# A seventh weight slot, another order at the first norm, and half of four key units formed earlier

## The chip, the cores and the metric

The kernel runs on one core of a Trainium2 chip. The metric is the time of one execution on the device, in microseconds; lower is better. All data is float32. A weight piece is 128 partitions by 4096 elements, 2.1 MB, and 140 such pieces make up nearly all of the 304.6 MB that the program moves.

## The reference

Two layers over 256 tokens of width 1024, with a condition vector `c` that gives every sub-layer its shift, scale and gate. Layer 0 attends with forgetting gates (16 heads), layer 1 with differential attention (8 heads of twice 64), and each is followed by a mixture of 16 experts, of which every token uses 2. After each of the four sub-layers comes a norm.

```python
def modulate(x, shift, scale):
    return x * (1.0 + scale[:, None, :]) + shift[:, None, :]

def post_norm_residual(x, y, gate, g, b):
    return layer_norm(DEEPNORM_ALPHA * x + (1.0 + gate[:, None, :]) * y, g, b)
...
    for l in range(DEPTH):
        mod = ada_params(c, ada_w[l], ada_b[l])      # silu(c) @ w + b
        sh_a, sc_a, g_a, sh_f, sc_f, g_f = jnp.split(mod, 6, axis=-1)
        ...                                          # h = modulate(x, sh_a, sc_a); y = attention(h) @ w_o
        x = post_norm_residual(x, y, g_a, ln_attn_g[l], ln_attn_b[l])
        h = modulate(x, sh_f, sc_f)
        m = grouped_moe(h, router_w, router_b, moe_w_gate[l], moe_w_up[l], moe_w_down[l])
        x = post_norm_residual(x, m, g_f, ln_ffn_g[l], ln_ffn_b[l])
```

## The kernel before

**The weights.** All weights come through `ring`, six slots of one piece each. The list `pieces` sets one order for the whole program: four pieces of the first modulation (`N_ADA[0]`), two of keys (`N_K`), then values, queries and further modulation pieces (the groups `ada` 1 to 6, of which group 3 is the first one of `kv_ada_w`), two of the output product (`N_WO`), then 48 expert pieces (`N_MOE`), six for each of eight pairs of experts: gate, up, gate, up, down, down. Layer 1 repeats this. SyncE's block walks through this list (`load`, `expert_loads`); before each piece it waits on `used` of the slot, which TensorE or VectorE raises after the last reader of the piece that lay there. SyncE works strictly in this order, so a piece that waits for its slot holds up all that stand behind it. Two more slots (`spare` and `stream`, slots 6 and 7) serve while experts run: the buffer `spare` holds the norm's gain and bias rows (`lnw`) at other times, and `stream` holds the residual `xres` and the normed rows `h`. Hence the seventh expert piece waits on `x_ready` and the eighth on `res_mm`, which says that TensorE has read the residual.

**The first modulation.** `first_modulation` on TensorE takes the four pieces of `N_ADA[0]` one after the other: strip matmuls (L1465), a copy by ScalarE or VectorE, four column matmuls (L1470), then `idle_work` (L1453), matmuls whose result nobody reads. After two pieces half of the modulation's columns are known, and half of `hT` (the modulated input, feature by token) is formed by ScalarE and VectorE; after four the other half. Then `turned_units` (L1529) forms eight key units of eight matmuls each.

**A norm and what follows.** VectorE forms the normed rows of block 0 and of block 1 (128 tokens each) and raises `xn_r` twice for each. TensorE turns them (`turn_stream`, L1506), ScalarE and VectorE modulate the turned blocks (`turned`, four of eight features each), and TensorE forms the router's logits and the positions (`route`). GpSimd's `gained` (L595, L596) multiplies the rows by the gain and adds the bias; it raises `x_ready` once for each block. In `route`, TensorE adds the residual of block 1 (`residual(l, 1)`, L1694) ahead of the two small matmuls (L1683, L1684) from which VectorE counts where each expert's tokens begin. From there on come the gather (L1705), the residual of block 0 and the experts. The gain and bias rows of norm 0 are loaded by `norm_rows(0)` ahead of the output weights.

**The experts.** `experts` on TensorE takes the pairs in turn: gate and up of one expert (L1724, L1725), then of the other, and down (L1732, L1733). An expert with more than 64 tokens runs `overflow` (from L1746 on) for the rest, 32 at a time; ScalarE, VectorE and TensorE hand the data to each other there.

**The way into layer 1.** `turn_stream(1)` starts with five of eight parts of `mod_product(4)` (L1431), which needs all four pieces of modulation group 4, the last pieces before the keys of layer 1. `turn_mod(4, 0)` (L1480) then turns its row into columns, and the eight key units of layer 1 follow.

## Time and profile before

| | us |
|---|---|
| median of three runs | 898.19 (897.6 to 899.9) |
| the profiled execution | 900.95 |
| its span, first to last instruction | 899.3 |
| TensorE busy | 834.7 (93%) |
| VectorE busy | 376.0 (42%) |
| ScalarE, GpSimd busy | 127.1, 90.3 |
| data moved | 304.59 MB, 339 GB/s over the span |

The rows are those of the profiled execution. Its time is 1.7 us above its span, and 2.8 us above the median of the three runs. A busy TensorE is not one at its peak, since matmuls are pipelined. The profile cuts the span into 40 slices of 22.5 us; the row of GB/s gives what the transfers moved in each. An instruction's line number is that of the kernel before, and `PE` is TensorE, `DVE` VectorE, `ACT` ScalarE, `POOL` GpSimd, `SPq` SyncE's queue.

### The profile page before, as it was taken

Reading aid. Unit: us, or ns where it says so; the run is one execution under the profiler, and the core shown is the slowest. Engines: PE = TensorE matmul, PEld = TensorE weight load, DVE = VectorE, ACT = ScalarE, POOL = GpSimd, SP = SyncE. Lnnn points to the kernel's source line nnn. Section 1 sums busy time; section 2 is a strip of 40 time slices with the busy share of each in tenths; the row PEclk is TensorE's granted clock in tenths of the full one; section 3 lists DMA queues with packets and bytes.
Section 4 is the critical chain, followed back from the end, with each engine's and each line's share of the span. In section 5 each row is a group of like instructions: output and inputs, shape, how many; then the busy total and the mean of one; then the engine's idle time right before and its main releaser. Section 6 shows DMA issues by size and latency. Waiting matters only on the chain.

```text
span 899.3 us, 10792 instructions
## 1 busy us (share of the span) xinstructions
PE 834.7 (93%) x3730; PEld 393.0 (44%) x3730; DVE 376.0 (42%) x927; ACT 127.1 (14%) x341; POOL 90.3 (10%) x146
## 2 busy tenths in 40 slices
PE   6899999999998998899979999999999999889984
PEld 3584675435333333333328557654533333333331
DVE  2185867475211221222148688828521122212215
ACT  1001243011100000000010114611110000010010
POOL 1000000051110001011004000215111110000000
PEclk9999999999999999999999999999999999999998
DMA  8999982019999999999999799405499999999901
GB/s 352 431 421 426 399 329 95 1 59 431 426 428 426 425 427 426 427 426 426 425 384 419 299 426 425 175 0 213 163 406 424 428 424 427 426 427 426 392 12 47
DMA packets 23408, 304.59 MB, mean 339 GB/s; under 512 B 2720, under 2 KB 3232, under 8 KB 5280
## 3 DMA queue, kind: packets, MB, share of 16 engines
q1 hardware_dynamic: 22752, 303.14, 80.6%
q8 instruction: 47, 0.77, 0.3%
q10 hardware_dynamic: 576, 0.40, 0.1%
q14 instruction: 33, 0.27, 0.1%
HBM read 302.49 MB, written 1.05 MB: 338 GB/s over the span
## 4 chain that ended last, share of the span: by engine, by line
PE 68%; DMA 21%; DVE 8%; issue 2%; POOL 1%; ACT 1%; POOLq 0%; DVEq 0%; ACTq 0%
PE ps L1724 17%; DMA ring<-in_moe_w_up_dram 12%; PE ps L1732 7%; PE ps L1558 6%; PE ps L1529 6%; PE ps L1542 6%; PE ps L1642 5%; PE ps L1737 4%; DMA stream<-in_moe_w_up_dram 3%; DMA ring<-in_ada_w_dram 3%; DMA ring<-in_moe_w_down_dram 3%; PE ps L1453 1%; PE ps L1431 1%; PE ps L1705 1%; PE ps L1465 1%
## 5 line engine op out<-in xcount | busy, mean ns | idle before, releaser
L1724 PE MATMUL ps<-ring,hT 128*64 128x512 f32 x384 | 172.4, 599 | 11.8 <-DMA ring<-in_moe_w_up_dram 9.9
L1725 PE MATMUL ps<-ring,hT 128*64 128x512 f32 x384 | 172.7, 600 | 0.0
L1233 DVE TENSOR_TENSOR arena<-arena,ps 128x256 f32<-128x256 f32 x32 | 13.5, 421 | 233.8 <-ACT arena L802 126.8
L1724 PEld LDWEIGHTS ps<-ring,hT 128*64 128x64 f32 x384 | 51.1, 138 | 117.4 <-issue 117.4
L1732 PE MATMUL ps<-ring,arena 128*64 128x512 f32 x208 | 94.8, 599 | 0.0
L1733 PE MATMUL ps<-ring,arena 128*64 128x512 f32 x208 | 94.8, 598 | 0.0
L414 DVE SCALAR_TENSOR_TENSOR spare<-ring,csig,spare 128x512 f32<-128x512 f32 x112 | 86.1, 769 | 3.8
L1737 PE MATMUL ps<-arena 128*128 128x512 f32 x144 | 66.6, 605 | 3.2 <-DVE arena L1242 3.2
L1724 PE MATMUL ps<-spare,hT 128*64 128x512 f32 x128 | 58.9, 609 | 2.7 <-DMA stream<-in_moe_w_up_dram 2.5
L1725 PE MATMUL ps<-stream,hT 128*64 128x512 f32 x128 | 58.9, 610 | 0.0
L1529 PE MATMUL ps<-hT,ring 128*128 128x256 f32 x256 | 57.2, 386 | 1.5 <-ACT hT L680 1.5
L630 POOL COPY hT<-arena 128x512 f32 x32 | 19.7, 615 | 372.6 <-PE ps L1725 222.1
L1242 DVE TENSOR_TENSOR arena<-ps,gbc 64x512 f32<-64x512 f32 x64 | 43.9, 686 | 29.6 <-PE ps L1733 28.6
L1542 PE MATMUL ps<-ring,hT 128*128 128x512 f32 x128 | 55.9, 595 | 0.0
L1529 PEld LDWEIGHTS ps<-hT,ring 128*128 128x128 f32 x256 | 49.6, 194 | 8.5 <-ACT hT L680 1.6
L1725 PEld LDWEIGHTS ps<-ring,hT 128*64 128x64 f32 x384 | 51.2, 138 | 0.0
L1732 PEld LDWEIGHTS ps<-ring,arena 128*64 128x64 f32 x208 | 26.3, 136 | 48.9 <-issue 48.9
L1737 PEld LDWEIGHTS ps<-arena 128*128 128x128 f32 x144 | 25.9, 189 | 43.7 <-issue 43.7
L799 ACT ACTIVATE arena<-ps 128x512 f32<-128x512 f32 x16 | 9.6, 597 | 243.4 <-PE ps L1725 243.4
L1542 PEld LDWEIGHTS ps<-ring,hT 128*128 128x128 f32 x128 | 24.1, 190 | 30.8 <-issue 30.8
L1724 PEld LDWEIGHTS ps<-spare,hT 128*64 128x64 f32 x128 | 17.3, 140 | 38.7 <-issue 38.7
L587 POOL TENSOR_SCALAR st<-mv 128x1 f32<-128x1 f32 x8 | 1.8, 223 | 294.6 <-DVE mv L1064 294.6
(281 smaller groups left out, 1083.3 us busy)
## 6 DMA issues: line engine op xcount, KB each, us to landing
ring<-in_moe_w_down_dram SPq DMA_DIRECT2D x26, 2048.0 KB, 21.8
ring<-in_ada_w_dram SPq DMA_DIRECT2D x24, 2048.0 KB, 14.7
ring<-in_moe_w_gate_dram SPq DMA_DIRECT2D x24, 2048.0 KB, 18.4
ring<-in_moe_w_up_dram SPq DMA_DIRECT2D x24, 2048.0 KB, 21.3
spare<-in_moe_w_gate_dram SPq DMA_DIRECT2D x8, 2048.0 KB, 23.2
stream<-in_moe_w_up_dram SPq DMA_DIRECT2D x8, 2048.0 KB, 25.3
ring<-in_fox_w_in_dram SPq DMA_DIRECT2D x6, 2048.0 KB, 9.8
ring<-in_kv_ada_w_dram SPq DMA_DIRECT2D x4, 2048.0 KB, 13.8
```

Of the source, the lines that this page charges most:

```text
L414: ins = alu.scalar_tensor_tensor(out=dst, in0=w[:, k, :], scalar=csig[:, k:k + 1], in1=dst, op0=ALU.mult, op1=ALU.add)
L630: link(g.tensor_copy(xw[:, j, :, 0:CAP], xsT[:, :, bass.ds(first, CAP)]))
L1242: d.tensor_tensor(out[lo:lo + CAP, half], ps[part_, bank, :], gbc[part_, 1, half], ALU.mult).then_inc(done, 1)
L1529: mm = t.matmul(ps[:, u % 4, 0:S], wcols(piece)[:, k, cc * P:(cc + 1) * P], src[:, k, :], start=(k == 0), stop=(k == KC - 1))
L1542: mm = t.matmul(ps[:, u % 4, :], hT[:, k, b * P:(b + 1) * P], wcols(piece)[:, k, :], start=(k == 0), stop=(k == KC - 1))
L1558: mm = t.matmul(ps[:, 7, 0:S], wcols(n)[:, k, (c % 4) * P:(c % 4 + 1) * P], src[:, k, :], start=(k == 0), stop=(k == KC - 1))
L1642: mm = t.matmul(ps[:, 2 * b + s_, :], oT[l][:, k, b * P:(b + 1) * P], wcols(n)[:, k, :], start=(k == 0), stop=(k == KC - 1))
L1724: t.matmul(ps[0:CAP, bank, :], lhs(k), wcols(ng)[:, k, :], start=(k == 0), stop=(k == KC - 1))
L1725: mm = t.matmul(ps[CAP:P, bank, :], lhs(k), wcols(nu)[:, k, :], start=(k == 0), stop=(k == KC - 1))
L1732: t.matmul(ps[0:CAP, bank, :], lhs(f), wdown(n)[:, f, 0:512], start=(f == 0), stop=(f == 3))
L1733: mm = t.matmul(ps[CAP:P, bank, :], lhs(f), wdown(n)[:, f, 512:D], start=(f == 0), stop=(f == 3))
L1737: return t.matmul(ps[:, 2 * b + q, :], lhs[:, b * P:(b + 1) * P], yy[:, q * 512:q * 512 + 512], start=False, stop=True, skip_group_check=True)
```

## The change

- The second piece of layer 0's output weights, `N_WO[0][1]`, no longer goes to the ring. It is loaded in four quarters into buffers that are free then: the two norm rows `lnw`, `h` of block 1, and `fold`. All ring slots behind it shift by one: the first expert piece takes the slot of the last query piece.
- The gain and bias rows of norm 0 would lie in two of these quarters, so `norm_rows(0)` moves from ahead of the output weights to behind the third expert piece. It waits until the quarters have been read.
- `gained` takes block 0 first, and waits for that block's rows alone; `residual` waits for `x_ready` in that order, so that block 1's residual waits for both. `number_slots` moves behind `gained`.
- Half of the first key piece is loaded after the first two modulation pieces (`key_halves`), and `early_keys` forms the first four of eight steps of four key units between the pieces, in the place of `idle_work`. `turned_units` then starts these four at step 4.
- `turned`: ScalarE modulates all eight features of block 0 and four of block 1, VectorE the last four of block 1.
- In front of layer 1, `mod_product(4)` is split in other places, `idle_work` stands first, and `turn_mod(4, 0)` comes after the first key unit.
- In `overflow`, the two turning matmuls stand ahead of the fold, and one product with `gate_halves` (formed once for each layer) takes the place of two with `gbc`.

```diff
     SPARES = 2
+    HALVES = RING + SPARES
     SLOT, TURN = [], []
-    turns, free = [0] * (RING + SPARES), list(range(RING))
...
-        s = free.pop(0)
+        s = HALVES if n == N_WO[0][1] else free.pop(0)
         SLOT.append(s)
         TURN.append(turns[s])
         turns[s] += 1
-        free.append(s)
+        if s != HALVES:
+            free.append(s)
 
     COLS_C, COLS_ADA, COLS_LN, COLS_NORMG, COLS_BF = 0, KC, KC + 7 * 2 * KC, KC + 7 * 2 * KC + 8 * KC, KC + 7 * 2 * KC + 8 * KC + 1
...
+    HT_N = ((4, 4), (16, 8), (28, 12), (36, 20), (48, 24))
     ARENA = 9690
 
...
+            return [lnw[:, 0, :], lnw[:, 1, :], h[:, 1, :], fold[:, :, :].rearrange("p a n -> p (a n)")]
+
+        def out_rows(n, q):
+
+            if SLOT[n] == HALVES:
+                return [a_.rearrange("p (k n) -> p k n", k=2) for a_ in quarter_pieces()[2 * q:2 * q + 2]]
+            return [wcols(n)[:, k:k + 2, :] for k in (4 * q, 4 * q + 2)]
+
         def wdown(n):
             return room(n).rearrange("p (k n) -> p k n", k=4)
 
...
+            def load_quarters(n):
+
+                for s_ in range(2):
+                    sp.wait_ge(ht_ready[s_], HT_N[0][s_])
+                sp.wait_ge(f_steps, 1)
+                for q, part_ in enumerate(quarter_pieces()):
+                    sp.dma_start(part_, pieces[n][:, 1024 * q:1024 * q + 1024]).then_inc(full[HALVES], 16)
+
             def load(n):
...
                         w = (moe_w_gate, moe_w_up, moe_w_down)[j % 2 if j < 4 else 2]
+                        if l == 0 and 6 * i + j == 3:
+                            spent(sp, N_WO[0][1])
+                            norm_rows(0)
...
                         sp.dma_start(room(n), w[l, e]).then_inc(full[SLOT[n]], 16)
+
+            def key_halves(q):
+
+                return room(N_K[0][0])[:, 2048 * q:2048 * q + 2048]
...
                     gate_bias(1)
-                if n == N_WO[0][0]:
-                    norm_rows(0)
                 if 2 <= n < RING:
                     landed(sp, n - 2)
-                load(n)
+                if n == 2:
+                    sp.dma_start(key_halves(0), pieces[N_K[0][0]][:, 0:2048]).then_inc(k_half, 16)
+                if n == N_K[0][0]:
+                    sp.dma_start(key_halves(1), pieces[n][:, 2048:4096]).then_inc(full[slot(n)], 16)
+                else:
+                    load(n)
             expert_loads(0)
             sp.wait_ge(xn_r, 4)
             gate_bias(2)
...
                 pool.wait_ge(lw_in, 32 * (norm + 1))
-                pool.wait_ge(xn_r, 4 * (norm + 1))
-                for b in (1, 0):
+                for b in range(NB):
+                    pool.wait_ge(xn_r, 4 * norm + 2 * b + 2)
                     link(g.tensor_tensor(xres[:, b, :], h[:, b, :], lnw[:, 0, :], ALU.mult))
                     g.tensor_tensor(xres[:, b, :], xres[:, b, :], lnw[:, 1, :], ALU.add).then_inc(x_ready, 1)
 
...
             inv_std(0)
+            gained(0)
             number_slots(0)
-            gained(0)
             windows(0)
...
                 spent(act, N_ADA[0][2 * half])
-                a.activation(parts[:, 2 * half, :], ps[:, 2 * half, :], ACT.Copy).then_inc(part_ev[0], 1)
+                a.activation(parts[:, 2 * half, :], ps[:, 6, :], ACT.Copy).then_inc(part_ev[0], 1)
                 first_turned(half)
 
...
                 act.wait_ge(cols_r, m + 2)
                 for b in range(NB):
-                    if m == 2 and b:
-                        mod_row_out(4)
-                    act.wait_ge(ht_mm, 4 * norm + 2 * b + 1)
-                    for k in range(4):
+                    for k in range(KC if b == 0 else 4):
+                        if k % 4 == 0:
+                            act.wait_ge(ht_mm, 4 * norm + 2 * b + k // 4 + 1)
                         modulated(hT[:, k, b * P:(b + 1) * P], turned_bank(b, k), m, k).then_inc(ht_ready[0], 1)
...
 
-                norm = M_NORM[m]
-                for b in range(NB):
-                    dve.wait_ge(ht_mm, 4 * norm + 2 * b + 2)
-                    for k in range(4, KC):
-                        modulated(hT[:, k, b * P:(b + 1) * P], turned_bank(b, k), m, k).then_inc(ht_ready[1], 1)
+                dve.wait_ge(ht_mm, 4 * M_NORM[m] + 4)
+                for k in range(4, KC):
+                    modulated(hT[:, k, P:2 * P], turned_bank(1, k), m, k).then_inc(ht_ready[1], 1)
 
...
                 landed(dve, n)
-                w = wcols(n)[:, 4 * q:4 * q + 4, :]
-                d.tensor_tensor(w, w, gbc[:, 0, 512 * s_:512 * s_ + 512].unsqueeze(1).broadcast_to([P, 4, 512]),
-                                ALU.mult).then_inc(wo_r, 1)
+                g_ = gbc[:, 0, 512 * s_:512 * s_ + 512].unsqueeze(1)
+                if SLOT[n] != HALVES:
+                    w = wcols(n)[:, 4 * q:4 * q + 4, :]
+                    d.tensor_tensor(w, w, g_.broadcast_to([P, 4, 512]), ALU.mult).then_inc(wo_r, 1)
+                    return
+                for at, w in enumerate(out_rows(n, q)):
+                    ins = d.tensor_tensor(w, w, g_.broadcast_to([P, 2, 512]), ALU.mult)
+                    if at:
+                        ins.then_inc(wo_r, 1)
+                    else:
+                        link(ins)
 
             def diff_norm(hd):
...
                     dve.wait_ge(ga_mm, KC * l + k + 1)
                     modulated(xsT[:, k, 0:NSLOT], ps[:, gather_bank(k), :], (1, 4)[l], k).then_inc(xs_ev[1], 1)
                 overflow_tables(l)
+                for q, rows in enumerate((slice(0, 64), slice(64, P))):
+                    link(d.tensor_copy(gate_halves[rows, :], gbc[rows, 1, 512 * q:512 * q + 512]))
                 for i in range(PAIRS):
                     n0 = N_MOE[l] + 6 * i
                     q = i + 8 * l
...
                         for strip in range(4):
-                            mm = t.matmul(ps[32 * strip:32 * strip + 32, at, :], crep[:, 2 * strip + k, :],
+                            mm = t.matmul(ps[32 * strip:32 * strip + 32, 6 + at % 2, :], crep[:, 2 * strip + k, :],
                                           wcols(n)[:, 2 * strip + k, :], start=(k == 0), stop=(k == 1))
                     mm.then_inc(used[slot(n)], 1)
                     pe.wait_ge(part_ev[at % 2], at // 2 + 1)
                     for kk in range(4):
-                        mm = t.matmul(ps[:, 4 + at, kk:kk + 1], parts[:, at, kk * P:(kk + 1) * P],
+                        one = 4 * (at // 2) + kk
+                        mm = t.matmul(ps[:, 4 + at % 2, one:one + 1], parts[:, at, kk * P:(kk + 1) * P],
                                       strips[:, 0:1], start=True, stop=True)
                     mm.then_inc(col_mm, 1)
-                    if at < 3:
-                        idle_work((4, 6, 3)[at], at + 1)
+                    if at == 0:
+                        idle_work(4, 7)
+                    if at == 1:
+                        idle_work(1, 3)
+                        for s_ in range(2):
+                            pe.wait_ge(ht_ready[s_], HT_N[0][s_] // 2)
+                        pe.wait_ge(k_half, 16)
+                        early_keys(range(3))
+                    if at == 2:
+                        early_keys(range(3, 4))
+
+            def early_keys(us):
+
+                for u in us:
+                    for k in range(KC // 2):
+                        t.matmul(ps[:, u, 0:S], wcols(N_K[0][0])[:, k, u * P:(u + 1) * P], hT[:, k, :],
+                                 start=(k == 0), stop=False)
 
             def turn_mod(gi, bank):
 
...
                 if norm == 1:
-                    mod_product(4, range(0, 5))
+                    idle_work(3, 7)
                 for b in range(NB):
                     if b and norm == 0:
                         mod_product(3, range(0, 2))
                     if b and norm == 1:
-                        mod_product(4, range(5, KC))
+                        mod_product(4, range(0, 3))
                     if b and norm == 2:
                         zeroed((0, 1, 0))
                     for s_ in range(2):
                         pe.wait_ge(xn_r, 4 * norm + 2 * b + s_ + 1)
-                        if norm == 1 and b and s_:
-                            pe.wait_ge(mod_row, 4)
                         for k in range(4 * s_, 4 * s_ + 4):
                             mm = t.transpose(turned_bank(b, k), h[:, b, k * P:(k + 1) * P], ident[:, :])
                         mm.then_inc(ht_mm, 1)
+                if norm == 1:
+                    mod_product(4, range(3, KC))
 
             def stream_turned(m):
...
                     for cc in range(4):
+                        if u == UNITS0 + 1:
+                            turn_mod(4, 0)
                         unit_free(u)
-                        for k in range(KC):
+                        for k in range(KC // 2 if u < 4 else 0, KC):
                             mm = t.matmul(ps[:, u % 4, 0:S], wcols(piece)[:, k, cc * P:(cc + 1) * P], src[:, k, :],
                                           start=(k == 0), stop=(k == KC - 1))
...
 
-                pe.wait_ge(x_ready, 2 * NB * l + 2 - b)
+                pe.wait_ge(x_ready, 2 * NB * l + b + 1)
...
                         with pe.Fori(b, b + n) as g:
-                            k = g * 8
+                            k = g * 7
                             pe.wait_ge(o_win, g + 1)
                             landed(pe, N_MOE[l] + 6 * i + 2 * j)
                             landed(pe, N_MOE[l] + 6 * i + 2 * j + 1)
                             gate_up_strips(i, j).then_inc(o_pe, 1)
+                            pe.wait_ge(o_dve, k + 3)
+                            for bb in range(NB):
+                                mm = t.transpose(ps[:, 7, bb * P:(bb + 1) * P], oput[:, bb, :], ident[:, :])
+                            mm.then_inc(o_pe, 1)
                             pe.wait_ge(o_act, g * 2 + 1)
-                            pe.wait_ge(o_dve, k + 3)
                             for q in range(4):
                                 mm = t.matmul(ps[:, 6, q * 2 * OCAP:(q + 1) * 2 * OCAP], ogu[:, q * P:(q + 1) * P],
                                               fold_strips[:, :], start=True, stop=True)
                             mm.then_inc(o_pe, 1)
...
             turn_stream(1)
             stream_turned(2)
-            turn_mod(4, 0)
```

In SyncE's queue, the pieces around the first experts stood so before (`kv_ada_w` is modulation group 3, `usedN` is the wait for slot N):

```order
L484 DMA ring<-in_kv_ada_w_dram 128x4096 [waits used3]
L511 DMA spare<-in_ln_attn_g_dram 128x1024
L511 DMA spare<-in_ln_attn_b_dram 128x1024
L484 DMA ring<-in_fox_w_o_dram 128x4096 [waits used4]
L484 DMA ring<-in_fox_w_o_dram 128x4096 [waits used5]
L498 DMA ring<-in_moe_w_gate_dram 128x4096 [waits used0]
L498 DMA ring<-in_moe_w_up_dram 128x4096 [waits used1]
L498 DMA ring<-in_moe_w_gate_dram 128x4096 [waits used2]
```

And now, in the same place:

```order
L508 DMA ring<-in_kv_ada_w_dram 128x4096 [waits used3]
L508 DMA ring<-in_fox_w_o_dram 128x4096 [waits used4]
L501 DMA spare<-in_fox_w_o_dram 128x1024 [waits f_steps,ht_ready_dve,ht_ready_act]
L501 DMA spare<-in_fox_w_o_dram 128x1024
L501 DMA stream<-in_fox_w_o_dram 128x1024
L501 DMA fold<-in_fox_w_o_dram 128x1024
L525 DMA ring<-in_moe_w_gate_dram 128x4096 [waits used5]
L525 DMA ring<-in_moe_w_up_dram 128x4096 [waits used0]
L525 DMA ring<-in_moe_w_gate_dram 128x4096 [waits used1]
L542 DMA spare<-in_ln_attn_g_dram 128x1024 [waits used8]
L542 DMA spare<-in_ln_attn_b_dram 128x1024
L525 DMA ring<-in_moe_w_up_dram 128x4096 [waits used2]
```

The norm rows have moved past both output pieces and three expert pieces, two of which wait for slots 0 and 1, where modulation group 3 lies.

On TensorE, between the second and the fourth piece of the first modulation, stood before:

```order
L1470 MATMUL ps<-strips,arena 128x1 x3
L1453 MATMUL ps<-maskf,ones 128x384 x6
L1465 MATMUL ps<-ring,crep 32x512 [waits full2]
L1465 MATMUL ps<-ring,crep 32x512 x7
L1470 MATMUL ps<-strips,arena 128x1 [waits part_ev_act]
L1470 MATMUL ps<-strips,arena 128x1 x3
L1453 MATMUL ps<-maskf,ones 128x384 x3
L1465 MATMUL ps<-ring,crep 32x512 [waits full3]
```

And now:

```order
L1512 MATMUL ps<-strips,arena 128x1 x3
L1494 MATMUL ps<-maskf,ones 128x384
L1530 MATMUL ps<-hT,ring 128x256 [waits k_half,ht_ready_dve,ht_ready_act]
L1530 MATMUL ps<-hT,ring 128x256 x11
L1506 MATMUL ps<-ring,crep 32x512 [waits full2]
L1506 MATMUL ps<-ring,crep 32x512 x7
L1512 MATMUL ps<-strips,arena 128x1 [waits part_ev_act]
L1512 MATMUL ps<-strips,arena 128x1 x3
L1530 MATMUL ps<-hT,ring 128x256 x4
L1506 MATMUL ps<-ring,crep 32x512 [waits full3]
```

Sixteen key matmuls (`hT,ring`) stand where eight of nine idle ones stood. In the trace each of these instructions has two records.

## Rows read from the trace of the kernel before

**Rows 1.** The page's row of data moved, one number for each of 40 slices.
```profile
GB/s 352 431 421 426 399 329 95 1 59 431 426 428 426 425 427 426 427 426 426 425 384 419 299 426 425 175 0 213 163 406 424 428 424 427 426 427 426 392 12 47
```

**Rows 2.** Stretches, window: length, busy us of PE, PEld, DVE, ACT, POOL, clock, DMA share, GB/s.
```profile
216.80:460.40 243.60, 224.70 (x986) 80.59 (x986) 55.99 (x136) 17.84 (x35) 20.00 (x35) 0.99 1.01 426
460.40:641.10 180.70, 174.10 (x759) 109.03 (x760) 125.48 (x301) 46.42 (x152) 30.56 (x39) 0.99 0.67 274
784.40:899.30 114.90, 96.29 (x450) 33.69 (x450) 31.22 (x66) 7.63 (x16) 7.31 (x14) 0.94 0.63 265
34.80:38.20 3.40, 3.02 (x7) 2.48 (x8) 0.78 (x4) 0.33 (x1) 0.00 (x0) 0.50 1.04 443
461.50:464.80 3.30, 3.30 (x23) 1.01 (x16) 1.32 (x2) 0.00 (x0) 0.00 (x0) 0.50 1.00 423
```

**Rows 3.** Timeline of SyncE's queue: start us, us, queue, line, transfer.
```profile
117.00 25.01 SPq L484 DMA_DIRECT2D ring<-in_fox_w_o_dram  x2
...
197.49 0.33 SPq L498 DMA_DIRECT2D ring<-in_moe_w_gate_dram  x1
...
215.91 0.33 SPq L498 DMA_DIRECT2D stream<-in_moe_w_up_dram  x1
224.82 0.33 SPq L498 DMA_DIRECT2D ring<-in_moe_w_gate_dram  x1
```

**Rows 4.** Line 498's transfer issued at 197.49 us.
```profile
DMA to landing us min/median/max: 7.4/7.4/7.4
```

**Rows 5.** Line 498's transfer issued at 224.82 us.
```profile
DMA to landing us min/median/max: 20.8/20.8/20.8
```

**Rows 6.** Timeline, GpSimd, 189 to 199 us: first and last of four gain products.
```profile
189.13 2.38 POOL L595 TENSOR_TENSOR stream<-stream,spare 128x1024 f32<-128x1024 f32 x1 [0.88 <-DVE stream L1072]
...
196.36 2.42 POOL L596 TENSOR_TENSOR stream<-stream,spare 128x1024 f32<-128x1024 f32 x1
```

**Rows 7.** Timeline, TensorE, 200 to 217 us.
```profile
200.95 1.88 PE L1694 MATMUL ps<-stream,identa 128*128 128x512 f32 x4
...
216.84 0.61 PE L1724 MATMUL ps<-ring,hT 128*64 128x512 f32 x1 [0.96 <-POOL hT L631]
```

**Rows 8.** The chain of waits, 9 to 40 us: start us, us, engine, line.
```profile
16.59 1.90 PE ps L1465 x16
...
20.31 3.98 PE ps L1453 x12
24.29 1.90 PE ps L1465 x16
...
27.91 2.04 PE ps L1453 x6
29.96 1.90 PE ps L1465 x16
```

**Rows 9.** Timeline, TensorE: the eight key units of layer 0.
```profile
35.18 29.37 PE L1529 MATMUL ps<-hT,ring 128*128 128x256 f32 x128 [1.51 <-ACT hT L680]
```

**Rows 10.** The chain of waits, 434 to 480 us.
```profile
433.99 26.35 DMA ring<-in_ada_w_dram
...
460.48 6.20 PE ps L1431 x40
466.67 1.02 PE ps L1506 x8
467.69 2.83 PE ps L1431 x24
...
473.52 0.63 PE ps L1480 x4
```

**Rows 11.** Timeline, VectorE: the last share of modulation group 5.
```profile
503.33 5.48 DVE L414 SCALAR_TENSOR_TENSOR spare<-ring,csig,spare 128x512 f32<-128x512 f32 x7
```

**Rows 12.** The chain of waits, 515 us: the sum over those shares.
```profile
515.52 1.00 PE ps L1446 x8
```

**Rows 13.** Waits of TensorE, 643 to 899 us: in total, times, longest.
```profile
PE ps L1724 <- DMA ring<-in_moe_w_up_dram: 3.0, 1, 3.0
```

**Rows 14.** The chain of waits, 844 to 875 us: the second of two gate products.
```profile
861.88 0.71 DVE arena L1271
```

**Rows 15.** Timeline, VectorE: the modulation products after norm 2.
```profile
616.67 2.63 DVE L898 TENSOR_SCALAR hT<-ps,modc 128x128 f32<-128x128 f32 x8
```

More of the change, by code:

```diff
@@ L105, in build @@
     SPARES = 2
+    HALVES = RING + SPARES
     SLOT, TURN = [], []
-    turns, free = [0] * (RING + SPARES), list(range(RING))
+    turns, free = [0] * (RING + SPARES + 1), list(range(RING))
     for n in range(len(pieces)):
@@ L251, in build @@
         ogu = mrow[:, 1, :]
-        full = [sem(f"full{i}") for i in range(RING + SPARES)]
-        used = [sem(f"used{i}") for i in range(RING + SPARES)]
+        full = [sem(f"full{i}") for i in range(RING + SPARES + 1)]
+        used = [sem(f"used{i}") for i in range(RING + SPARES + 1)]
         res_mm = sem("res_mm")
@@ L830, in _ @@
             turned(2)
+            mod_row_out(4)
             us = proj_units(1)
@@ L1269, in overflow @@
                             dve.wait_ge(o_pe, g * 5 + 4)
-                            for q, rows in enumerate((slice(0, 64), slice(64, P))):
-                                d.tensor_tensor(oy[rows, :], ps[rows, 7, :], gbc[rows, 1, 512 * q:512 * q + 512],
-                                                ALU.mult).then_inc(o_dve, 1)
+                            d.tensor_tensor(oy, ps[:, 7, :], gate_halves, ALU.mult).then_inc(o_dve, 1)
                             dve.wait_ge(o_pe, g * 5 + 5)
```

39 lines of the change are left out of this document (21 added, 18 removed).

## The prediction

> **What bounds the kernel now.** I read the data moved by slice first, then the stretches, then SyncE's queue, and only then the chain of waits. The row of GB/s [rows 1] shows three kinds of time: transfers at about 426 GB/s, a gap in the slices from 135 to 202 us (95, 1 and 59), and another in layer 1. From 216.8 to 460.4 us the 16 DMA engines are busy for the whole stretch (share 1.01, 426 GB/s) while TensorE leaves 19 of 243.6 us free [rows 2]: layer 0's experts are bound by transfers, and one piece takes 2.1 MB / 426 GB/s = 4.9 us. Layer 1's attention (460.4 to 641.1 us) moves only 274 GB/s and keeps TensorE busy: that stretch, like layer 0's attention, belongs to TensorE. In layer 1's experts TensorE waits only once for weights, 3.0 us [rows 13].
>
> So a change counts here if it lets the transfers of layer 0's experts start earlier or run without a hole, or if it shortens TensorE's chain elsewhere. SyncE's queue shows why they start late: between the output weights (117.00 and about 25 us later) and the first expert piece (197.49) no transfer is issued, since all six slots are taken until TensorE has finished modulation group 3 [rows 3].
>
> **The first modulation.** Before, the strips of its second to fourth piece start at 16.59, 24.29 and 29.96 us, and the first key unit at 35.18 [rows 8, 9]. From the last strips to that unit is 5.2 us; the same way for the first half puts the first four features of `hT` at 16.59 + 5.2 = 21.8 us. The eight units are 64 matmuls, 128 records in 29.37 us, so 0.46 us for a matmul. Twelve early ones run from 21.8 to 27.3, so the third piece's strips start at 27.3 in place of 24.29. The key half ahead of it costs the piece 1.05 MB / 426 GB/s = 2.5 us; it was there by 24.29, so now by 26.8, which is hidden. To the fourth piece it was 5.67 us, of which 2.04 idle matmuls; with four key matmuls (1.8) in their place its strips start at 27.3 + 5.5 = 32.8. It was there by 29.96 and so now by 32.5. The first unit starts at 38.0, and 48 matmuls are left, 22.0 us: 60.0 in place of 64.55. That is 4.5 us. I take 4.0, as the transfers behind are no earlier than before and run at their limit up to about 110 us [rows 1]. Bounds: 0, if the added waits eat it, and 6.0, if TensorE isn't at the lower clock here, which it was from 34.8 to 38.2 us (0.50, so 1.2 GHz) [rows 2].
>
> The quartered output piece makes four products of two; a product over 128x512 takes 0.71 us [rows 14], and the elements are as many as before, so it costs between 0 and 0.7 us, and I take 0.2. TensorE's release of modulation group 3, and with it the first issues of expert weights, comes at 197.49 - 4.0 + 0.2 = 193.7 us.
>
> **The seventh slot and the norm rows.** The first expert piece now lands in the gap, which is worth 4.9 us. But the gain and bias rows stand behind two pieces that wait for slots 0 and 1, so they too are issued after 193.7. A piece issued into an empty queue lands 7.4 us later [rows 4]: pieces two and three at 201.1 and 206.0, the rows (1.05 MB, 2.5 us) at 208.5. GpSimd's four products took from 189.13 to 196.36 + 2.42, 9.65 us [rows 6], and end at 218.2. `residual(0, 1)` now waits for both blocks, and it stands on TensorE ahead of the counting matmuls. It ran at 200.95 [rows 7] and will run at 218.2: 17.2 us later. Behind it are queued the counts, the gather, the second residual and all experts; nothing of the router's chain on VectorE can pass. The first expert matmul moves from 216.84 [rows 7] to 234.1.
>
> TensorE stands still for some 20 us there. After the one long wait in front of layer 1 it ran at 0.50, 1.2 GHz, in 461.5 to 464.8 us [rows 2]. From the old residual to the first expert lie 15.9 us of which about two thirds are matmuls; running all of these at half speed would add up to 10 us, none 0. I take 2.5, nearest to a spell like the 3.3 us of that row with some work behind it, and get 236.6. The Trainium skill ("TensorE: Matmul & The Clock Gate", section "What's actually happening") has it that the throttled clock is the default and sustained activity releases it. By that rule the restart is slow, as in the row at 461.5; without it the sum below would come to -1.0 in place of +1.5.
>
> The eight slots hold pieces one to eight; the ninth needs the first one's slot. TensorE gave that back 224.82 - 216.84 = 7.98 us after the first expert matmul [rows 3, 7], so now at 244.6. By then the queue has run dry (eight pieces' work ended long before; the eighth waits for `res_mm`, 215.91 [rows 3], now 235.7, and lands at 243.1). The ninth lands at 244.6 + 7.4 = 252.0. Before, it landed 20.8 us after 224.82, at 245.6 [rows 3, 5]. From there on both versions are bound by transfers of the same number: TensorE needs about 26 us for six pieces and the transfers 29.4, and it has caught up before the end. So layer 0's weights end 6.4 us later, although 4.0 + 4.9 us were put in ahead. Of the 19 us that TensorE had free, most are used up.
>
> **In front of layer 1.** The last piece of modulation group 4 landed at 433.99 + 26.35 = 460.34, and the first key unit started at 473.52 + 0.63 = 474.15, 13.8 us later [rows 10]. Now only the 64 instructions of the modulation (6.20 + 2.83) and one block's turns (1.02) stand in between, 10.05 us: 3.8 us less, with `turn_mod`'s 0.63 paid after the first unit: -3.2. The new `idle_work` lies in the wait. The cover: VectorE's shares of group 5 stay tied to their transfers, and the last ends at 508.8, against 515.52 where TensorE reads them [rows 11, 12]; 6.7 - 3.2 = 3.5 us of slack are left. If that is gone, up to 3.2 us come back.
>
> **The small ones.** `overflow` loses one 0.71 us product on the way of TensorE [rows 14]. Two such runs of layer 1 lie behind the last wait for weights, so -1.4, and the moved turns another -0.1. The one in layer 0 isn't at the bound. Four of the eight VectorE products of 2.63 us after a norm [rows 15] move to ScalarE, 1.3 us at most; TensorE fills most of that time with other matmuls, so I take 0.2 for norm 2. Norm 2's gain products start earlier, but TensorE has eight idle matmuls (`zeroed`) ahead of that residual: 0.
>
> **The sum** against the profiled execution (900.95 us, span 899.3): +6.4 - 3.2 - 1.5 - 0.2 = +1.5 us. On the median of the three runs, 898.19, that is 899.7.
>
> **The rivals.** (1) The seventh slot pays. If the norm rows landed soon after their issue, not behind two pieces, `x_ready` would come at about 210 and the ninth piece at 243; if nothing waited at all, at 239. The totals are then -7.5 and -11.5 us, 890.7 and 886.7. For it: the rows are small. Against it: a transfer into a filled queue landed after 20.8 us, one into an empty queue after 7.4 [rows 4, 5], so they take turns, and the program's order puts the rows behind slots 0 and 1 whatever the queue does. (2) Slower, by the restart. Every microsecond that TensorE's way from the residual to the first returned slot loses is a microsecond of the whole, since the transfers then wait for it. It decides from 1.2 us above my 2.5; at the lower clock for half of that way it costs 5.5, so 902.7, and for all of it 10, so 907. For it: 20 us of standing still, followed by short matmuls with waits between them. Against it: in the two rows at 0.50 one short spell was all. (3) Somewhat faster: no slow spell at the restart and none in the key units, -2.5 - 2.0 on my sum, 895.2.
>
> **How the numbers follow.** This kernel's measurement can tell about 0.3%, 2.7 us. My forecast with its neighbourhood, 896 to 902, has a chance of 0.52; the slower restart beyond that 0.30; rival (3) 0.10; rival (1) 0.08. Within the first case some weight is past +2.7 (above 900.9), so: faster 0.14, within 0.3% 0.48, slower 0.38. The likeliest case's own range is 896 to 903. The range for 8 in 10 reaches to rival (3) and to the half of the slow restart: 893.5 to 905.
>
> **What would show it.** In the changed profile: no matmul to speak of on TensorE from about 197 to 218 us, its residual waiting for GpSimd, and GpSimd waiting for the norm rows' transfer until about 208; a first expert piece landed by 150; the first expert matmul near 236; a hole in the transfers at about 230 to 245; the first key unit at 38, the units' end at 60; 10 us from the last piece of group 4 to layer 1's first key unit. I am wrong if that residual doesn't wait, if TensorE can't catch up with the transfers before 460 us, or if the shares of group 5 become a wait.

## The result, and the profile after

The changed kernel takes 907.49 us (median of 11 runs, 903.96 to 912.62) against 899.6 of the kernel before in the same comparison (11 runs, 895.35 to 904.95): ratio 1.0091, 95% interval 1.0065 to 1.0117. It is slower, and outside my range of 893.5 to 905. The profiled execution took 911.69 us (span 910.0; before 900.95 and 899.3), so 10.7 us are to be found.

The page's rows of clock, DMA share and data moved, in 40 slices:

```profile
PEclk9899999995999999989999999999999999999988
DMA  9999992039499999999998899505289999999901
GB/s 353 403 421 429 400 369 94 1 125 421 175 431 425 427 425 426 427 421 427 423 426 366 356 427 414 210 1 217 104 351 427 425 428 425 426 426 428 422 39 47
```

The slice at about 228 to 250 us, 426 before [rows 1], moves 175: a hole that was not there. SyncE's queue (columns as in [rows 3]) shows how it comes about:

```profile
140.88 0.33 SPq L525 DMA_DIRECT2D ring<-in_moe_w_gate_dram  x1
196.59 0.33 SPq L525 DMA_DIRECT2D ring<-in_moe_w_up_dram  x1
196.96 0.43 SPq L525 DMA_DIRECT2D ring<-in_moe_w_gate_dram  x1
197.44 0.43 SPq L542 DMA_DIRECT2D spare<-in_ln_attn_g_dram  x1
...
221.22 0.33 SPq L525 DMA_DIRECT2D spare<-in_moe_w_gate_dram  x1
238.26 0.33 SPq L525 DMA_DIRECT2D stream<-in_moe_w_up_dram  x1
247.16 0.33 SPq L525 DMA_DIRECT2D ring<-in_moe_w_gate_dram  x1
```

One expert piece is issued in the gap. The other two wait for their slots until 196.59, and only then come the norm rows. The ninth piece goes out at 247.16, before at 224.82. GpSimd and TensorE's waits from 200 to 475 us:

```profile
211.72 2.34 POOL L629 TENSOR_TENSOR stream<-stream,spare 128x1024 f32<-128x1024 f32 x1 [24.42 <-DMA spare<-in_ln_attn_b_dram]
...
218.86 2.34 POOL L630 TENSOR_TENSOR stream<-stream,spare 128x1024 f32<-128x1024 f32 x1
```

```profile
PE ps L1754 <- POOL stream L630: 21.0, 1, 21.0
PE ps L1816 <- DMA ring<-in_moe_w_down_dram: 2.3, 1, 2.3
```

GpSimd waits for the bias row's transfer, and TensorE's residual waits 21.0 us for GpSimd. This wait is called the hold from here on. The stretches (columns as in [rows 2]) show the same hole, and the lower clock beside it:

```profile
198.00:221.00 23.00, 2.21 (x6) 0.66 (x4) 1.17 (x8) 0.00 (x0) 9.12 (x4) 0.60 0.99 412
221.00:240.00 19.00, 17.09 (x56) 10.89 (x58) 11.62 (x40) 4.39 (x5) 2.85 (x5) 0.85 0.55 222
203.00:226.60 23.60, 5.35 (x13) 3.29 (x14) 0.67 (x4) 0.00 (x0) 9.84 (x5) 0.50 1.01 423
```

Followed along the program, the changed kernel is later than before by: -0.9 us at SyncE's first issue behind modulation group 3; +20.3 at `residual(0, 1)` (221.25); +22.3 at the first expert matmul (239.19); +9.4 at the landing of modulation group 4's last piece (469.70), as the transfers' free time in layer 0 is used up; +8.3 at the end of layer 1's key units (510.06); +13.1 at layer 1's second residual (654.08); +10.7 at the end.

The rise from 8.3 to 13.1 is at norm 2. Here VectorE's normed rows and GpSimd's gain products, first of the kernel before, then of the changed one:

```profile
615.60 1.15 DVE L1072 TENSOR_SCALAR stream<-stream,mv,st 128x512 f32<-128x512 f32 x2 [1.08 <-POOL st L588]
```

```profile
616.89 2.36 POOL L595 TENSOR_TENSOR stream<-stream,spare 128x1024 f32<-128x1024 f32 x1 [0.88 <-DVE stream L1072]
```

```profile
623.88 4.98 DVE L1112 TENSOR_SCALAR stream<-stream,mv,st 128x512 f32<-128x512 f32 x2 [1.08 <-POOL st L622]
```

```profile
623.75 2.34 POOL L629 TENSOR_TENSOR stream<-stream,spare 128x1024 f32<-128x1024 f32 x1
626.16 2.41 POOL L630 TENSOR_TENSOR stream<-stream,spare 128x1024 f32<-128x1024 f32 x1
628.94 2.35 POOL L629 TENSOR_TENSOR stream<-stream,spare 128x1024 f32<-128x1024 f32 x1 [0.36 <-DVE stream L1112]
```

Before, GpSimd starts once VectorE has finished. Now it starts 0.13 us ahead of it, and the same two VectorE instructions take 4.98 us, not 1.15. Each lasts until a GpSimd product has ended (626.09, 628.58) and 0.3 us more. No row calls this a wait: it is hidden in the duration. TensorE's turns hang on it. They wait 1.90 and 1.84 us for these rows, and a stretch at 0.50 follows (629.45 to 632.87 us), in which four idle matmuls take 3.57 us, where four take 1.88 us in the kernel before:

```profile
626.42 0.66 PE L1561 MATMUL ps<-ident,stream 128*128 128x128 f32 x4 [1.90 <-DVE stream L1112]
628.92 0.66 PE L1561 MATMUL ps<-ident,stream 128*128 128x128 f32 x4 [1.84 <-DVE stream L1112]
629.41 3.57 PE L1760 MATMUL ps<-arena,ones 128*128 128x512 f32 x4
```

So the loss at norm 2 has two parts: the rows, 3.8 us longer, and the lower clock behind them, 1.4 us between the rows' end and the router's first matmul (4.05 us, before 2.70), for which the idle matmuls have to end. The steps behind that are 0.3 us shorter than before.

### The profile page after: what moved, and what is told of

It reads as the page before. It is cut to its first block, busy times and chain, and to the rows that moved or that the text cites. A ratio compares the mean times of both kernels' runs of the same rounds, so it can differ in the third digit from the quotient of the medians.

```text
span 910.0 us, 10780 instructions
## 1 busy us (share of the span) xinstructions
PE 838.6 (92%) x3720; PEld 393.6 (43%) x3720; DVE 370.3 (41%) x918; ACT 131.5 (14%) x353; POOL 90.9 (10%) x146
## 3 DMA queue, kind: packets, MB, share of 16 engines
HBM read 302.49 MB, written 1.05 MB: 334 GB/s over the span
## 4 chain that ended last, share of the span: by engine, by line
PE 82%; DMA 7%; DVE 6%; POOL 2%; issue 1%; ACT 1%; SPq 0%; POOLq 0%; DVEq 0%; ACTq 0%
PE ps L1784 22%; PE ps L1792 11%; PE ps L1617 6%; PE ps L1797 6%; PE ps L1601 6%; PE ps L1588 6%; PE ps L1701 5%; DMA ring<-in_moe_w_up_dram 3%; DMA ring<-in_moe_w_down_dram 3%; DMA spare<-in_ln_attn_b_dram 2%; PE ps L1472 1%; PE ps L1760 1%; PE ps L1765 1%; PE ps L1845 1%; PE ps L1871 1%
## 5 line engine op out<-in xcount | busy, mean ns | idle before, releaser
L428 DVE SCALAR_TENSOR_TENSOR spare<-ring,csig,spare 128x512 f32<-128x512 f32 x112 | 84.2, 752 | 3.8
L1588 PE MATMUL ps<-hT,ring 128*128 128x256 f32 x224 | 52.0, 395 | 1.5 <-ACT hT L714 1.5
L1588 PEld LDWEIGHTS ps<-hT,ring 128*128 128x128 f32 x224 | 44.3, 199 | 8.9 <-ACT hT L714 1.6
```

The lines of the kernel that those rows point to most:

```text
L428: ins = alu.scalar_tensor_tensor(out=dst, in0=w[:, k, :], scalar=csig[:, k:k + 1], in1=dst, op0=ALU.mult, op1=ALU.add)
L1588: mm = t.matmul(ps[:, u % 4, 0:S], wcols(piece)[:, k, cc * P:(cc + 1) * P], src[:, k, :], start=(k == 0), stop=(k == KC - 1))
```

## The experiments

All ratios are to the kernel before, in runs on the same chip, with 95% intervals.

**Norm rows first.** In `expert_loads(0)`:

```
-                        if l == 0 and 6 * i + j == 3:
+                        if l == 0 and 6 * i + j == 1:
                             spent(sp, N_WO[0][1])
                             norm_rows(0)
```

> The changed kernel, with the two norm rows issued as soon as the output piece in the seventh slot is spent (about 185 us), ahead of expert pieces two and three in SyncE's program, not behind them. Theory (the hold in front of the experts): the rows land near 193, GpSimd's four products end near 202, residual(0, 1) runs at 201 to 203 instead of 221.3, the first expert matmul at 217 to 219 instead of 239.2, the last piece of modulation group 4 lands at 454 to 457 instead of 469.7; total 892 to 896, so 12 to 15 us below the changed kernel and a few us below the kernel before. Rival 1 (the loss is TensorE's lower clock, whatever the rows do): the residual moves but the total stays within 4 us of 907. Rival 2 (layer 0's experts are now TensorE's own bound): the weights' end moves by less than 5 us, total 901 or more.

Measured: 893.74 us, ratio 0.9933 (0.9905 to 0.9962); faster than both kernels. SyncE's queue:

```profile
184.48 0.33 SPq L542 DMA_DIRECT2D spare<-in_ln_attn_g_dram  x1
...
196.40 0.33 SPq L525 DMA_DIRECT2D ring<-in_moe_w_up_dram  x1
...
224.81 0.33 SPq L525 DMA_DIRECT2D ring<-in_moe_w_gate_dram  x1
```

The residual runs at 199.86, the first expert at 216.83, group 4 ends at 454.11, 15.6 us earlier. Both rivals fall. The seventh slot gives its piece's time once nothing holds: 454.11 against 460.34 before is 6.2 us, of which 1.1 are the earlier first issue (196.40, before 197.49) and 5.1 the piece. This is read from the traces; no run has the seventh slot as its only change.

**The norm order undone.** GpSimd's blocks in the order (1, 0) after all four halves, `number_slots` ahead of `gained`, `residual` waiting on `2 * NB * l + 2 - b`.

> The changed kernel with the norm order undone: GpSimd numbers the slots first and takes block 1 before block 0 after all four normed quarters are there, and residual(l, 1) waits for one block alone. Theory: at norm 0 residual(0, 1) needs two products less, 4.7 us, so 216.5 in place of 221.3 and layer 0's end 4 to 5 us earlier; at norm 2 VectorE's two normed rows of block 1 take 1.1 us again, not 5.0, and the router starts 4 to 5 us earlier; together 8 to 10 us, total 897.5 to 900. Rival 1 (only the hold behind pieces two and three counts, norm 2's long rows are made up for later): 4 to 5 us, 903. Rival 2 (clock): within 2 us of 907.5.

Measured: 899.46, ratio 0.9993 (0.9974 to 1.0012). The residual runs at 215.27, group 4 ends at 463.70 (469.70), and norm 2's rows take 1.15 us again. Both parts count. Of the 6.0 us at the residual 4.5 belong to the order: the first issue behind modulation group 3 was itself 1.5 us earlier in this trace (195.08).

**One line of it.**

```
-                for b in range(NB):
-                    pool.wait_ge(xn_r, 4 * norm + 2 * b + 2)
+                pool.wait_ge(xn_r, 4 * (norm + 1))
+                for b in range(NB):
```

> The changed kernel with one line altered: GpSimd's gain products wait for all four normed quarters, and so don't start beside VectorE's normed rows of block 1; the blocks' order and its place ahead of the slot numbers stay. Theory (GpSimd's products and VectorE's normed rows hold each other up at norm 2): the rows take 1.1 us in place of 5.0, the router of layer 1 starts 4 to 5 us earlier against the end of the attention, nothing changes at norm 0 where the rows' transfer is last; total 902.5 to 904. Rival (the long rows come from something else, or the gain is eaten by the later products, which residual(1, 1) now waits for): total within 1.5 us of 907.5.

Measured: 904.4, ratio 1.0046 (1.0025 to 1.0067), 4 us less than the changed kernel's ratio gives. Layer 0 is unaltered (group 4 ends at 469.73), and VectorE's two rows are short:

```profile
623.50 1.00 DVE L1112 TENSOR_SCALAR stream<-stream,mv,st 128x512 f32<-128x512 f32 x2 [1.08 <-POOL st L622]
```

**Both** (called the mixture below): norm rows first, norm order undone.

> Both: the norm rows issued ahead of pieces two and three, and the norm order undone. Theory, by the sum of the two: residual(0, 1) near 200, as in the kernel before, the first expert near 216, the last piece of modulation group 4 at 454 to 456, norm 2 without the stretch: 888 to 891, so 9 to 11 us below the kernel before (ratio 0.988 to 0.990). Rival (the two gains are not additive, since TensorE becomes the bound of layer 0's experts once the hold is gone): 893 to 896.

Measured: 888.56, ratio 0.9880 (0.9850 to 0.9910). The gains of the rows' place (0.0158 of the ratio) and of norm 2 (0.0045, from the run with one line altered) add up: 0.9888 is their sum. The part of the norm order that lay in the hold goes with the hold.

**Late rows in the kernel before.** No seventh slot; `norm_rows(0)` is taken from ahead of the output weights and put behind the third expert piece.

> The kernel before, with one thing of the change and no seventh slot: its two norm rows are issued behind the first three expert pieces, not ahead of the output weights. Theory (the hold alone makes the loss in layer 0): the rows land near 215, GpSimd's first two products end near 219.5, residual(0, 1) runs there in place of 200.95, TensorE runs at the lower clock around it, the ninth piece is issued at 243 to 246 in place of 224.8 and group 4's last piece lands at 466 to 470 in place of 460.3; total 6 to 10 us above the kernel before, 906 to 910. Rival (the loss came from the quartered piece in the seventh slot or from the new pieces' order): the hold is caught up by the experts' end, total within 2 us of 900.

Measured: 909.26, ratio 1.0090 (1.0063 to 1.0117): this one move makes a loss as large as the whole change.

```profile
195.84 0.33 SPq L500 DMA_DIRECT2D ring<-in_moe_w_gate_dram  x1
...
197.16 0.51 SPq L513 DMA_DIRECT2D spare<-in_ln_attn_g_dram  x1
...
246.51 0.33 SPq L500 DMA_DIRECT2D ring<-in_moe_w_gate_dram  x1
```

The residual runs at 220.78 and group 4 ends at 469.10. The early expert piece of the changed kernel is worth nothing while the hold is there.

**The new norm order alone, in the kernel before.**

> The kernel before with the norm order of the change alone: GpSimd takes block 0 as soon as its two halves are normed, ahead of the slot numbers, and residual(l, 1) waits for both blocks. The norm rows are there early, so here the products can meet VectorE's normed rows of block 1 at both norms. Theory (they hold each other up wherever they meet): the two rows take 4 to 5 us in place of 1.1 at norm 0 (near 187 us) and at norm 2 (near 616 us); TensorE's last product of modulation group 3, and with it the first issue of expert weights, comes 3 to 5 us later than 197.5, and the total rises by 7 to 10 us, to 907 to 910. Rival 1 (only norm 2 has it): 4 to 5 us, 904 to 905. Rival 2 (the long rows of the changed kernel came from the other edits): within 1.5 us of 900.

Measured: 909.5, ratio 1.0115 (1.0084 to 1.0145). With the rows there early, the two engines meet at norm 0 as well; VectorE's and GpSimd's rows there:

```profile
188.99 4.97 DVE L1072 TENSOR_SCALAR stream<-stream,mv,st 128x512 f32<-128x512 f32 x2 [1.07 <-POOL st L588]
```

```profile
188.85 2.34 POOL L595 TENSOR_TENSOR stream<-stream,spare 128x1024 f32<-128x1024 f32 x1
191.27 2.41 POOL L596 TENSOR_TENSOR stream<-stream,spare 128x1024 f32<-128x1024 f32 x1
```

The first expert weights go out at 203.96, 6.5 us later than before; I had expected 3 to 5. Of the 6.5 us 1.2 were there before the norm (188.99 against 187.83, first column of these rows; the key units of layer 0 had ended 1.2 us later, at 65.72), and 3.8 are the rows. A stretch at 0.50 (191.0 to 197.8 us) that begins in the middle of this may be the last 1.5; I didn't test that. At norm 2 the same rows are as long and no stretch at 0.50 follows; from their start to the second residual it takes 3.5 us more than before, not 4.9.

**The lower clock around the hold.** Two runs. In the first I meant to fill the hold with matmuls on zeros, and put them in a wrong place:

```
                 pe.wait_ge(tot_r, l + 1)
                 zeroed((1, 1))
+                if l == 0:
+                    zeroed((1,) * 11)
```

> The changed kernel with eleven more matmuls on zeros (1.86 us each, 20.4 us) on TensorE ahead of residual(0, 1), so that it is busy through the hold; the hold itself stays. Theory (the restart's lower clock is a small part of the loss): no stretch at 0.50 from 202 to 226 us, residual(0, 1) still at 221.3, the first expert matmul 1.5 to 2.5 us earlier than 239.2, and layer 0's end as much: total 905 to 906. Rival (the lower clock is most of the loss): 6 us or more, total 901.5 or less.

Measured: 916.97, ratio 1.0186 (1.0160 to 1.0212). They stood behind the residual, not ahead of it as the expectation says, so this run tells nothing of the clock. But it is a dose of the other step: TensorE's way from the residual to the first returned slot is made longer. First expert +6.8 us against the changed kernel (246.04), ninth issue +6.8 (254.01), group 4's end +6.8 (476.54). In each of the six kernels with the hold that end comes 222.5 to 222.8 us after the ninth issue; in the kernel before, whose queue was full, 235.5.

In the second they are in the hold:

```
                 if l == 0:
                     mod_product(3, range(4, KC))
-                    zeroed((6, 7, 6, 7))
+                    zeroed((6, 7) * 13)
```

> The changed kernel with 22 more matmuls on zeros directly ahead of residual(0, 1), 0.93 us each by the row of the four that stand there (3.70 us), so 20.5 us: TensorE is busy through the hold, and the hold itself stays. (In hold_busy eleven of them stood behind that residual, 10 us of work on the way to the first expert.) Theory (the restart's lower clock is a small part of the loss): residual(0, 1) stays at 219 to 221.5, no stretch at 0.50 around it, the first expert matmul 17 to 18 us behind it rather than 17.9 plus, so 1.5 to 3 us earlier than in the changed kernel against its residual (239.19 - 221.25 = 17.9, before 15.9), and layer 0's end as much: total 904 to 906. Rival (the lower clock is most of the loss): 901.5 or less.

Measured: 906.08, ratio 1.0073 (1.0049 to 1.0096). The stretch is at full clock, and the residual still waits:

```profile
198.00:220.00 22.00, 19.75 (x47) 8.51 (x46) 0.00 (x0) 0.00 (x0) 9.53 (x5) 1.00 1.02 425
```

```profile
195.02 22.58 PE L1760 MATMUL ps<-arena,ones 128*128 128x512 f32 x52
219.86 1.98 PE L1754 MATMUL ps<-stream,identa 128*128 128x512 f32 x4 [2.25 <-POOL stream L630]
```

From residual to first expert it is 15.8 us, as before the change (15.9), not 17.9. So, in the traces, the lower clock costs 2.1 of the 22.3 us, and the wait itself the rest. In time the run is not told apart from the changed kernel (1.0073 and 1.0091, the intervals overlap), but it is far from the 901.5 us or less that the rival asked for.

**Parts of the mixture undone.** Early key units: the key piece comes whole, the idle matmuls are back, all eight units run behind the modulation. The line that forms them:

```
-                        for k in range(KC // 2 if u < 4 else 0, KC):
+                        for k in range(KC):
```

> The faster mixture (norm rows first, old norm order) without the early key units: the first key piece comes whole, TensorE's idle matmuls are as in the kernel before, and all eight units run behind the first modulation. Theory (the transfers behind the key units take up their gain): the units end 1 to 6 us later than the mixture's 63.3 or at the same time, but TensorE's last matmul of modulation group 3 comes only 0.5 to 1.5 us later, and so does the end: 889 to 890.5 against 888.6. Rival (my forecast's term, 4 us of units are 4 us of the whole): 892 to 893.

Measured: 889.87, ratio 0.9871 (0.9848 to 0.9893), the same as the mixture's 0.9880. The units end at 64.4 (63.3), the first issue is at 197.38 (196.34): what little the early units gain in the mixture's trace, 1.1 us, arrives in full, and the run doesn't test what becomes of a larger gain. The other traces do. Up to 1.7 us ahead of the kernel before the first issue follows the units' end (the units 1.2 us ahead and the issue 1.3 in the run with one line altered, both 1.7 with the late rows). With the units 4.1 to 6.4 us ahead (the two runs for the hold, and the norm order undone), the first issue was only 2.2 to 2.4 us ahead.

The work in front of layer 1 in its old order (the first lines of the edit):

```
                 if norm == 1:
-                    idle_work(3, 7)
+                    mod_product(4, range(0, 5))
...
```

> The faster mixture with the work in front of layer 1 in its old order: modulation group 4's products in bank 7 around the first block's turns, ScalarE's row before the second block, VectorE's fold of group 3 and turn_mod before the first key unit. Theory: the mixture starts its first key unit 10.3 us after group 4's last piece has landed, the kernel before 13.8; undone it is 13 to 14 again, less 0.6 for turn_mod, so the total rises by 2.5 to 4 us, to 891 to 892.5. Rival (VectorE's shares of group 5 hang on their transfers and take it back): 888 to 889.5.

Measured: 892.0, ratio 0.9912 (0.9890 to 0.9933). The intervals overlap; the trace has the key units' end 39.7 us after group 4's last piece, in the mixture 38.6, where it is 36.6 when TensorE arrives early enough (norm rows first). So the trace shows 1.1 us of the 2.5 to 4 that I expected, and the time can't settle it.

The overflow's steps as before:

> The faster mixture with the overflow's steps as before: two down products of 64 rows, and the turned places behind the folded strips. Theory: 0.7 us a round for the second product and up to 0.5 for the order; two rounds of layer 1 stand at TensorE's bound and layer 0's ones partly, so 1.4 to 3 us in all, 890 to 891.5. Rival (other matmuls cover it): within 0.7 us of 888.6.

Measured: 890.65, ratio 0.9892 (0.9863 to 0.9920): not told from the mixture by time. In the traces the first round of layer 1, with no lower clock in it, takes 12.24 us undone and 11.19 with the change, so 1.05 us a round.

**The mixture with its first gaps filled:** `idle_work(2, 3)` ahead of the early key units, and after the fourth piece `idle_work(2, 6)`.

> The faster mixture with three idle matmuls more in the first modulation: one ahead of the early key units and two ahead of the others, in TensorE's gaps of 0.8 and 1.5 us. Theory: what is gained there lies in front of transfers that run back to back, so at most 1.3 us reach the first issue of expert weights even if the two stretches at 0.50 (21.4 and 38.5 us) go: 887 to 889, same as the mixture's 888.6 within its spread. Rival (the gaps bring the lower clock, and it costs the whole 5 us): 884 to 885.

Measured: 887.29, ratio 0.9850 (0.9823 to 0.9877), the lowest, though its interval overlaps the mixture's. No stretch at 0.50 is left before 84 us, and the key units end at 58.1, where I had forecast 60.0. TensorE's and VectorE's rows:

```profile
20.94 5.45 PE L1532 MATMUL ps<-hT,ring 128*128 128x256 f32 x24
...
37.13 20.99 PE L1590 MATMUL ps<-hT,ring 128*128 128x256 f32 x96
...
74.82 7.13 PE L1603 MATMUL ps<-ring,hT 128*128 128x512 f32 x16 [0.35 <-DMA ring<-in_fox_w_in_dram]
85.02 10.05 PE L1603 MATMUL ps<-ring,hT 128*128 128x512 f32 x16 [3.06 <-DVE arena L1016]
```

```profile
79.78 0.49 DVE L426 TENSOR_SCALAR spare<-ring,csig 128x512 f32<-128x512 f32 x1 [4.54 <-DMA ring<-in_ada_w_dram]
80.30 2.33 DVE L428 SCALAR_TENSOR_TENSOR spare<-ring,csig,spare 128x512 f32<-128x512 f32 x3
...
84.74 0.22 DVE L1016 COPY arena<-arena 72x128 f32<-72x128 f32 x1
```

The units end at 58.1, 6.4 us ahead of the kernel before. But VectorE waits 4.54 us for a modulation piece, forms half of its share, and only then the forget gate (L1016), for which TensorE waits 3.06 us. The first issue comes at 197.76, no earlier than before (in this run a stretch at 0.50 from 84.1 us stretches the next units from 7.13 to 10.05). In the run with the norm order undone, which had no lower clock there either, the units also ended at 58.2 and the first issue came at 195.08: of 6.4 us, 2.4 were left. That these waits for the transfers are what takes the rest is read from the rows; no run removes them.

## Why the prediction was wrong

**The hold was right in kind and nearly in size.** Residual behind the slots' release: +24.5 us forecast (218.2 - 193.7), 24.7 measured. From there to the first expert 18.4 against 17.9, clock 2.5 against 2.1, to the ninth issue 8.0 against 8.0. That the transfers never catch up from there was right too (group 4 ends 214.8 us after the ninth's landing before, 215.2 now). I had taken that end at +6.4; it came at +9.4, because all of it counts from the first issue.

**The first step that failed: "That is 4.5 us. I take 4.0, as the transfers behind are no earlier than before".** The sentence names the reason and then discounts it by 0.5. Measured: -0.9. The two parts of the error: in the changed kernel's trace the key units ran partly at 0.50 (38.9 to 45.8 us; their 96 records took 23.90 us, not 20.99), and so did the early ones (21.9 to 25.3 us; 24 records in 6.96 us, not 5.43), so they ended only 0.8 us earlier; and where they ran at full clock, 4.0 of 6.4 us were lost behind them, where the transfers had no free time [rows 1]. By the run without these stretches the first issue would have been 2.4 us earlier at full clock, and not 3.8: 1.4 us of the error are the way behind the units, 1.5 the clock. I asked whether the key pieces were there in time, but not what VectorE does with the pieces behind them. The sum's error from this is +3.0.

**The second: "Norm 2's gain products start earlier ... : 0".** It cost 4.9 us in the trace, a stretch at the lower clock included; in time, altering that one line gives back 0.45% or 4 us. I looked at who waits for the products (nobody, behind `zeroed`), not at what they run beside. The trace of before shows the effect. Its chain of waits has

```profile
196.59 2.35 DVE rc L1118
```

beside GpSimd's product of 196.36 [rows 6], and in the changed kernel, where GpSimd is idle at that time, the same step (L1158, 194.63 us) takes 0.29. The Trainium skill states the rule ("SBUF — State Buffer", section "SBUF: two separate sides"): VectorE, in its two-port modes or with two inputs from SBUF, and GpSimd lock a shared pair of ports for a whole instruction; whichever starts first has it, and the other one blocks. By that rule each of the two rows ends one short step behind one of GpSimd's products; the trace agrees (0.28 us behind 626.09 and behind 628.58), though no row names the mode of these rows. With the 4.9 us in the sum the forecast would have been 904.6.

**Third, in front of layer 1: "-3.2".** Measured: -1.1. The 10.05 us were counted from the last piece's landing, as if TensorE were ready then, which it was before. After the hold TensorE itself is late. Its waits for weights in layer 0 are down to one of 2.3 us (at 384.7), and group 4's last piece (469.70) finds it at the experts' end:

```profile
466.58 3.67 PE L1797 MATMUL ps<-arena 128*128 128x512 f32 x8 [1.61 <-DVE arena L1282]
470.08 2.10 PE L1494 MATMUL ps<-maskf,ones 128*128 128x384 f32 x6
...
477.29 4.50 PE L1472 MATMUL ps<-ring,crep 128*32 128x512 f32 x40
481.72 3.72 PE L1588 MATMUL ps<-hT,ring 128*128 128x256 f32 x16
```

The idle matmuls (L1494), meant for the wait, run behind it, and the first key unit starts 12.0 us after the landing. Where it is early, the edit gives more than I took: first key unit 8.3 us after the landing with the norm rows first, 13.8 before. The shares of group 5, the cover that I had named, did not become a wait: VectorE had them at 518.7, and TensorE read them at 523.7.

**The overflow, "-1.5":** 1.05 us a round in the trace for a round at full clock, two rounds in layer 1. Their sum can't be read from the changed kernel, whose last round met a stretch at 0.50 (868.4 to 875.2) and took 14.08 us, before 13.83. All behind norm 2 gave -2.4, of which some 1.6 are such a stretch of the kernel before (785.7 us) that isn't there now. Such stretches come and go between the traces, so I call that part luck.

The four differences, +3.0, +2.1, +5.1 and -0.9, make up the 9.2 us between the forecast sum of +1.5 and the +10.7 measured, but for rounding.

**The rivals.** Rival (2), slower, had the right sign, 902.7 to 907, for the wrong reason: it put the price on the clock after the hold, and 2.1 us of clock is all there was behind it. Rival (1), the seventh slot pays, did not come about in this kernel: the rows, issued at 197.44 and 197.91, landed at 210.1 and 211.7, as the main case had it. What it said would follow if nothing waited can be compared with the experiments: the ninth piece at 239 and -11.5 us. With the norm rows first it landed at 239.4, and the time by the ratio was -6.0 us with norm 2's loss in it; with the norm order undone as well it landed at 239.3, and the time was -10.8.

## What to carry to other kernels

When a load moves behind others in a queue, its place costs what those others wait for, not their bytes: here two small rows behind two waiting pieces cost all that the slot gained and more, and moving them up two places turned a loss of 0.9% into a gain of 0.7%. Before an instruction of GpSimd is moved earlier, look at what VectorE runs at that time; a block shows as long durations, not as waits. A gain on TensorE in front of transfers that run back to back may be worth only its first part: here 1.7 us passed whole, and of 6.4 us 2.4 were left.

## What the hardware showed beside this

The lower clock came and went between executions of the same code: the two early stretches at 0.50 (about 21.5 to 25 and 38.5 to 45.5 us) were there in six of the nine profiled kernels whose first modulation is the changed kernel's; two had only one, at 37.5 and 37.8 us for 3.4 us, and one had none. The 96 records of the key units behind the modulation then took 20.99, 22.6 or 23.9 us. A few per mille between single traces are of this kind, which is why the terms above name the stretches that lie in them.
